# Value projections of the mixers and the retention, computed token by token with the activations stationary

## The reference, cut to what matters

```python
# first block, layer 1: retention, 4 heads, dv = 512, latent and context tokens (512 in all)
p = h @ w_in
q, k, v, g = split(p)                     # v: (heads, tokens, 512)
scores = einsum('bhid,bhjd->bhij', q, k) * intra
y = einsum('bhij,bhje->bhie', scores, v) + ...
# second block, both layers: mixer
hq, hf, hi, hg, aq, ak, av, ga, gb = split(h @ w_in[l])
v_a = hi.reshape(b, t, 8, 128)            # values of the gated scan (hgrn2)
v_b = heads(av)                           # values of 3 x 4 attention heads of width 128
o_a = hgrn2_chunk_scan(q_a, k_a, v_a, log_f)
o_b = sum over groups of alpha * (softmax(q_b k_b^T) v_b)
```

## Time and profile before

| | |
|---|---|
| runs | 3542.81, 3546.66, 3550.40 us; median 3546.66 |
| profiled execution | 3541.26 us, of which the span in the profile is 3539.5 |
| busy | PE 3431.8 us, DVE 2032.4, ACT 1268.4, POOL 640.2 |
| DMA | 507.9 MB, queue share 48.7% |
| mean granted TensorE clock | 0.99 |

### The profile page before, as it was taken

One profiled execution on the slowest core, in us unless ns is written; L12 is line 12 of the kernel. 1 busy time (PEld: TensorE's weight loads), 2 busy tenths in 40 slices (PEclk: granted clock), 3 DMA queues, 4 the chain that ended last, 5 costly groups with the idle time before them and its releaser, 6 DMA issues.

```text
span 3539.5 us, 55525 instructions
## 1 busy us (share of the span) xinstructions
PE 3431.8 (97%) x22315; PEld 3109.0 (88%) x22315; DVE 2032.4 (57%) x2374; ACT 1268.4 (36%) x1678; POOL 640.2 (18%) x535
## 2 busy tenths in 40 slices
PE   7999999999999999999999999999999999998999
PEld 4888878888888888888999999989999999998999
DVE  3766836657766535545555456855545455864644
ACT  2222223212232124333434344355444444355443
POOL 2212303202221130002222220000323230000222
PEclk9999999999999999999999999999999999999999
DMA  5645504545355433334654654334565655343664
GB/s 195 189 149 155 161 22 123 173 140 175 107 172 167 130 97 89 90 95 140 184 173 140 182 166 138 108 114 131 158 183 165 184 167 155 108 120 93 177 184 143
DMA packets 862994, 507.89 MB, mean 143 GB/s; under 512 B 15060, under 2 KB 843024, under 8 KB 862800
## 3 DMA queue, kind: packets, MB, share of 16 engines
q1 hardware_dynamic: 862432, 503.74, 48.7%
q0 software_dynamic: 368, 1.38, 0.1%
HBM read 504.01 MB, written 1.05 MB: 143 GB/s over the span
## 4 chain that ended last, share of the span: by engine, by line
PE 87%; DVE 5%; ACT 4%; issue 2%; DMA 1%; POOL 0%; SPq 0%; DVEq 0%; POOLq 0%; ACTq 0%
PE bank L578 26%; PE bank L580 25%; PE bank L579 25%; ACT whi_all L1023 2%; PE bank L946 2%; PE bank L589 1%; DVE wlo_all L1271 1%; DVE t_full L1406 1%; PE bank L661 1%; PE bank L800 1%; PE bank L761 1%; PE bank L748 1%; PE bank L850 1%; PE bank L845 1%; DMA raw<-in_w_branch_a 1%
## 5 line engine op out<-in xcount | busy, mean ns | idle before, releaser
L1271 DVE TENSOR_TENSOR wlo_all<-raw,whi_all 128x1024 fp32r<-128x1024 f32 (+3 forms) x768 | 1015.1, 1323 | 972.1 <-ACT whi_all L1023 970.8
L578 PE MATMUL bank<-xn_hi,whi_all 128*128 128x256 f32 (+1 forms) x4608 | 1481.2, 321 | 18.6 <-DVE xn_lo L1395 11.4
L579 PE MATMUL bank<-xn_lo,whi_all 128*128 128x256 f32 (+1 forms) x4608 | 1447.4, 314 | 0.0
L580 PE MATMUL bank<-xn_hi,wlo_all 128*128 128x256 f32 (+1 forms) x4608 | 1447.2, 314 | 0.0
L1023 ACT CAST whi_all<-raw 128x1024 fp32r<-128x1024 f32 (+3 forms) x768 | 836.5, 1090 | 1032.6 <-PE bank L580 988.4
L578 PEld LDWEIGHTS bank<-xn_hi,whi_all 128*128 128x128 f32 x4608 | 882.6, 192 | 83.6 <-DVE xn_lo L1395 13.5
L580 PEld LDWEIGHTS bank<-xn_hi,wlo_all 128*128 128x128 f32 x4608 | 881.8, 191 | 52.3
L579 PEld LDWEIGHTS bank<-xn_lo,whi_all 128*128 128x128 f32 x4608 | 883.0, 192 | 49.5
L578 PE MATMUL bank<-h_hi,whi_all 128*128 128x256 f32 (+1 forms) x1408 | 459.0, 326 | 1.2 <-POOL h_lo L1767 1.2
L580 PE MATMUL bank<-h_hi,wlo_all 128*128 128x256 f32 (+1 forms) x1408 | 454.7, 323 | 0.0
L579 PE MATMUL bank<-h_lo,whi_all 128*128 128x256 f32 (+1 forms) x1408 | 454.4, 323 | 0.0
(11 more groups left out here) (247 smaller groups left out, 2802.2 us busy)
## 6 DMA issues: line engine op xcount, KB each, us to landing
raw<-in_ffn_w_in SPq DMA_DIRECT2D x176, 512.0 KB, 3.9
raw<-in_w_in SPq DMA_DIRECT2D x168, 512.0 KB, 3.8
ada_w<-in_ada_w SPq DMA_DIRECT2D x128, 512.0 KB, 4.0
raw<-in_ffn_w_gate SPq DMA_DIRECT2D x88, 512.0 KB, 3.8
raw<-in_ffn_w_up SPq DMA_DIRECT2D x88, 512.0 KB, 3.9
raw<-in_ffn_w_down SPq DMA_DIRECT2D x32, 768.0 KB, 5.2
raw<-in_ret_w_in SPq DMA_DIRECT2D x48, 512.0 KB, 3.8
raw<-in_ffn_w_out SPq DMA_DIRECT2D x32, 768.0 KB, 5.4
```

Source lines behind the costliest of these rows:

```text
L578: pe.matmul(o, whi[s][:, k, :], hi, start=(k == 0), stop=False)
L579: pe.matmul(o, whi[s][:, k, :], lo, start=False, stop=False)
L580: return pe.matmul(o, wlo[s][:, k, :], hi, start=False, stop=(k == ks - 1))
L1271: tt(wlo[s][:, 0:ks, :], raw[s][:, 0:ks, :], whi[s][:, 0:ks, :].bitcast(F32), ALU.subtract).then_inc(lo_done[s], 1)
```

## The change

- In `ret_v`, `hi` and `att_v` the 128x128 activation blocks are stationary and the weights of two neighbouring slots move together (2 x 128 columns). A pair of slots gives, per token tile, 256 output columns with the tokens on the partitions.
- A pair starts when both slots are ready, and its 48 products (96 in the retention) run before `mm_done` of either slot is signalled. The last product is cut into two of 128 columns, each of which signals one slot.
- In the mixer the first half of a pair's products (k = 0 to 3) is issued in the even unit and the second half in the odd one.
- ACT copies each bank straight to the values' final place. `r_vf`, `vfm`, all transposes of values, their copies and their semaphores are gone. Waits that they carried are put elsewhere. The order of all other side steps is as it was.

```diff
-        for n in range(5):
-            put(HI + 4 * n + 4, "turn", n)
...
+            def pair_ready(s, r):
+                slot_ready(s - 1, r)
+                slot_ready(s, r)
+
+            def values_mm(s, blocks, hi, lo, tiles):
...
+                two = slice(s - 1, s + 1)
+                for t, k in blocks:
+                    b, c0 = s - 1 + 2 * t // tiles, t % (tiles // 2) * 2 * P
+                    o = bank[b][:, c0:c0 + 2 * P]
+                    tok = slice(t * P, (t + 1) * P)
+                    pe.matmul(o, hi[:, k, tok], whi_all[:, two, k, :], start=(k == 0), stop=False)
+                    pe.matmul(o, lo[:, k, tok], whi_all[:, two, k, :], start=False, stop=False)
+                    if (t, k) != (tiles - 1, DC - 1):
+                        pe.matmul(o, hi[:, k, tok], wlo_all[:, two, k, :], start=False, stop=(k == DC - 1))
+                        continue
+                    for i in range(2):
+                        pe.matmul(o[:, i * P:(i + 1) * P], hi[:, k, tok], wlo_all[:, s - 1 + i, k, :], start=False,
+                                  stop=(i == 1)).then_inc(mm_done[s - 1 + i], 1)
...
-                    linear(f"ret_v{h}", pair(xn_hi, xn_lo, 512), 512)
-
-                    pe.wait_ge(rt["vf"], 4 * (h + 1))
-                    for t in range(4):
...
-                        for e in range(4):
-                            mm = pe.transpose(bank[4 + t][:, e * P:(e + 1) * P], r_vf[:, e, t * P:(t + 1) * P], ident[:])
-                        mm.then_inc(rt["vt"], 1)
+                    for s in (1, 3):
+                        pair_ready(s, phases[f"ret_v{h}"]["first"])
+                        values_mm(s, [(t, k) for t in range(4) for k in range(DC)], xn_hi, xn_lo, 4)
...
+                    if ph in ("hi", "att_v"):
+                        blocks = [(t, k) for k in range(DC) for t in range(2)]
+                        if s % 2:
+                            values_mm(s, blocks[DC:], xn2_hi, xn2_lo, 2)
+                        else:
+                            pair_ready(s + 1, p["first"] + it)
+                            values_mm(s + 1, blocks[:DC], xn2_hi, xn2_lo, 2)
+                        return
...
-                def turn(i):
...
-                        for s in range(SLOTS):
-                            mm = pe.transpose(bank[6 + t][:, s * P:(s + 1) * P], vfm[:, s, t * P:(t + 1) * P], ident[:])
...
-                        act.copy(r_vf[:, s, :], bank[s][:]).then_inc(rt["vf"], 1)
-                        act.wait_ge(rt["vf"], 4 * h + s + 1)
-                        act.nop().then_inc(bank_free[s], 1)
+                        i = s % 2
+                        act.copy(r_v[:, 2 * i:2 * i + 2, (s - i) * P:(s - i + 2) * P],
+                                 bank[s][:].rearrange("p (t e) -> p t e", t=2)).then_inc(bank_free[s], 1)
...
-                        act.copy(vfm[:, s, :], bank[s][:, 0:SEQ]).then_inc(att["vf"], 1)
...
+                        n, t = n0 + c // SLOTS, s % 2
+                        dst = g_v(t, n) if n < 2 else a_v[t][:, n - 2, :, :]
+                        act.copy(dst[:, s - t:s - t + 2, :], bank[s][:, 0:SEQ].rearrange("p (c e) -> p c e", c=2))\
+                            .then_inc(bank_free[s], 1)
...
-                    for t in range(4):
-                        dve.wait_ge(rt["vt"], 4 * h + t + 1)
-                        dve.tensor_copy(r_v[:, t, :], bank[4 + t][:]).then_inc(rt["v"], 1)
```

More of the change, by code:

```diff
@@ L188, in mixer_order @@
         side = [[] for _ in units]
-        QK, HI, HG = 16, 40, 60
+        QK, HG = 16, 60
         def put(u, *item):
@@ L330, in build @@
         r_k = at("r_k", [P, 2, 512], 82)
-        r_vf = at("r_vf", [P, 4, 512], 86)
         r_yn = at("r_yn", [P, 2, 512], 86)
@@ L356, in build @@
         a_qk = at("a_qk", [P, 24, SEQ], 76)
-        vfm = at("vfm", [P, 4, SEQ], 100)
         a_s = at("a_s", [P, 1152], 104)
@@ L428, in build @@
         f_a, f_ae, f_aed, f_b, f_hi, f_lo = [sem(f"four_{n}") for n in ("a", "a_sb", "a_sb_dve", "b", "hi", "lo")]
-        rt = {k: sem(f"ret_{k}") for k in ("qk", "kctx", "vf", "vt", "v", "dm", "expo", "s", "p", "y", "var", "root",
+        rt = {k: sem(f"ret_{k}") for k in ("qk", "kctx", "dm", "expo", "s", "p", "y", "var", "root",
                                            "yn", "yt", "z", "zlo")}
-        att = {k: sem(f"att_{k}") for k in ("vf", "vt", "v", "sq", "ss", "rt", "rr", "sp", "tk", "rope", "s", "mx",
+        att = {k: sem(f"att_{k}") for k in ("sq", "ss", "rt", "rr", "sp", "tk", "rope", "s", "mx",
                                             "ex", "rs", "p", "pt", "pte", "o", "ohi", "olo")}
@@ L790, in do_retention @@
                     pe.wait_ge(rt["kctx"], 2 * (h + 1))
-                    pe.wait_ge(rt["v"], 4 * (h + 1))
                     for j in range(4):
+                        if h:
+                            pe.wait_ge(rt["yn" if j < 2 else "z"], 2 * h)
                         for c in range(2):
@@ L796, in do_retention @@
                         mm.then_inc(rt["s"], 1)
+                    for s in range(SLOTS):
+                        pe.wait_ge(bank_free[s], phases[f"ret_v{h}"]["first"] + 2)
                     pe.wait_ge(rt["p"], 4 * (h + 1))
@@ L859, in sum_, with values_taken @@
                     row_sum(c % 12, 11, 7, a_sq[c % SLOTS], att["ss"])
[L861 to L867, removed]
+                def values_taken(ph):
+                    p = phases[f"{ph}{l}"]
+                    for s in range(SLOTS):
+                        pe.wait_ge(bank_free[s], p["first"] + p["rounds"] + 1)
                 def spread(i):
                     pe.wait_ge(att["rr"], 2 * l + i // 6 + 1)
-                    bank6_free()
+                    if 12 * l + i:
+                        pe.wait_ge(att["tk"], 12 * l + i)
                     row_spread(2 * i % 12, 6, 0, a_rr[i // 6])
                     row_spread(2 * i % 12 + 1, 6, 1, a_rr[i // 6]).then_inc(att["sp"], 1)
-                    spreads[0] += 1
-                def turn(i):
[L878 to L883, removed]
-                        for s in range(SLOTS):
-                            mm = pe.transpose(bank[6 + t][:, s * P:(s + 1) * P], vfm[:, s, t * P:(t + 1) * P], ident[:])
-                        mm.then_inc(att["vt"], 1)
-                    turns[0] += 2
                 def scores(hh):
@@ L892, in scores @@
                         pe.wait_ge(att["rope"], 12 * (l + 1))
-                        pe.wait_ge(att["v"], 10 * (l + 1))
                         pe.wait_ge(hg["oe"], 4 * (l + 1))
@@ L925, in attend @@
                         pe.wait_ge(hg["hm"], 4 * (l + 1))
+                        values_taken("att_v")
                     if n:
@@ L962, in values @@
                         pe.wait_ge(hg["xe"], 4 * (l + 1))
-                        pe.wait_ge(att["v"], 10 * l + 4)
+                        values_taken("hi")
                     for h in range(4 * half, 4 * half + 4):
@@ L976, in hsum @@
                     pe.wait_ge(hg["oe"], 4 * l + 4)
-                    pe.wait_ge(att["v"], turns[0])
+                    pe.wait_ge(att["rt"], 2 * (l + 1))
                     for h in range(HH):
@@ L987, in hspread @@
                     row_spread(2 * j + 1, 7, 1, g_rr[:]).then_inc(hg["sp"], 1)
-                steps_ = dict(unit=unit, sum=sum_, spread=spread, turn=turn, scores=scores, turn_probs=turn_probs,
+                steps_ = dict(unit=unit, sum=sum_, spread=spread, scores=scores, turn_probs=turn_probs,
                               attend=attend, pairs=pairs, cross=cross, values=values, hsum=hsum, hspread=hspread)
@@ L1128, in values @@
                         if h and s == 0:
-                            act.wait_ge(rt["yt"], 2 * h)
-                            act.wait_ge(rt["zlo"], h)
-                        act.copy(r_vf[:, s, :], bank[s][:]).then_inc(rt["vf"], 1)
-                        act.wait_ge(rt["vf"], 4 * h + s + 1)
-                        act.nop().then_inc(bank_free[s], 1)
+                            act.wait_ge(rt["y"], 2 * h)
+                        i = s % 2
+                        act.copy(r_v[:, 2 * i:2 * i + 2, (s - i) * P:(s - i + 2) * P],
+                                 bank[s][:].rearrange("p (t e) -> p t e", t=2)).then_inc(bank_free[s], 1)
                     stream(f"ret_v{h}", values)
@@ L1160, in evacuate @@
                     def evacuate(s, c, r):
-                        n = 5 * l + n0 + c // SLOTS
-                        if s == 0 and n:
-                            act.wait_ge(att["vt"], 2 * n)
-                        act.copy(vfm[:, s, :], bank[s][:, 0:SEQ]).then_inc(att["vf"], 1)
-                        act.wait_ge(att["vf"], 4 * n + s + 1)
-                        act.nop().then_inc(bank_free[s], 1)
+                        n, t = n0 + c // SLOTS, s % 2
+                        dst = g_v(t, n) if n < 2 else a_v[t][:, n - 2, :, :]
```

(6 more changed lines are left out.)

## The result

| | before | after |
|---|---|---|
| median of the runs | 3545.19 us (4 runs) | 3569.28 us (4 runs, 3567.89 to 3574.10) |
| ratio to before | | 1.0068, 95% interval 1.0051 to 1.0086 |
| span of the profiled execution | 3539.5 | 3566.9 (+27.4) |
| u40 to u61, layer 0 / layer 1 | 102.1 / 100.3 | 113.7 / 114.1 |
| retention, heads 1 to 3, each | 68.0 | 66.9 |

The account below looks back on a forecast made before the run. TensorE was taken as the bound, busy 97%, with DVE and ACT close behind in the mixer. Retention -4.1 and mixers +32.6 gave +28.5 us, so 3575 us on the median, range 3548 to 3598.

Parts of the forecast that it names:

- The central claim: Mixer: DVE and ACT run close behind TensorE, so when they may start can matter more than TensorE's work.
- Rivals 1 and 3: Whole kernel: not slower because side steps have slack, 3515 us, chance 0.11; new matmul form dear, 3598 or above, chance 0.09.
- Retention, -4.1: Four retention heads: removed stretch -2.55, narrower matmuls +1.28, cut halves +0.24, so -1.03 us a head.
- Here the pairs should wait for nothing: Retention: pairs of slots find their splits done in time, so no waiting time was added.
- Turns and their waits, 7.7 a layer: Mixer, removed per layer: five turns of 8 transposes, 4.3 us, and two waits for ACT's copies, 1.8 and 1.6.
- gaps 22.9: Mixer, per layer: eight new TensorE waits for late ACT and DVE side steps, 22.9 us together.
- E+1.84: Mixer: DVE's lo of the even slot starts 1.84 us after the pair's end on TensorE.
- u54: Mixer: spread 9 waits for bank 6 from rope 8, behind squares(1) on ACT, a gap of 3.7 us.
- The halves: Last product of a pair cut into two of 128 columns, 0.12 us each, adding 0.12 a pair.
- four falls added and two taken off: Mixer, per layer: clock falls of 1.8 us each, four new ones 7.2 us, two removed ones 3.6.
- Mixers forecast +32.6: Both mixer layers: gaps 22.9, clock 7.2 and halves 1.2, less 15.0 removed, +16.3 us a layer.
- Rival 2: Mixers: gaps come but half as large, 15 instead of 30 us a layer, 3545 us; chance 0.10.

Follow-up runs that it names:

- mix_only: The changed kernel with the retention's part of the diff taken back, so only the mixers have the new form; 3570.27 us, 1.0071 of the kernel before.
- late_signal: The kernel before, with mm_done of even slots in hi and att_v signalled only near the end of the odd unit; 3601.06 us, ratio 1.0153.
- defer: The changed kernel with ACT's and DVE's even units in hi and att_v done at the odd units; 3531.68 us, 0.9965 of the kernel before.
- defer_h0: defer, with DVE splitting slot 1 before the rope at ret_qk of head 0; 3528.26 us, 0.9955 of the kernel before.
- defer_dve: The changed kernel with even units in hi and att_v put off to the odd ones on DVE alone; 3542.49 us, 0.9993 of the kernel before.

## Why the prediction was right, and where it was off

**What bounds.** The central claim held: a change of when ACT and DVE may start matters more than a change of TensorE's work. mix_only puts the loss in the mixers; late_signal makes it from the old matmuls by the signal alone; defer undoes it with the new matmuls and the signal left as it is. Rivals 1 and 3 are out: the gaps came, and the pace is 0.119.

**Retention, -4.1: measured -1.1.** Heads 1 to 3 are each 1.11 us shorter (68.03 to 66.92 from scores to scores), where I had 1.03. The failed step is "Here the pairs should wait for nothing", for head 0. There ret_qk runs across its four slots, so all four mm_done come within a few microseconds of the end, and the pair needs slot 1, whose split stands behind the rope. From the end of the crossed part to the scores, head 0 takes 38.9 us instead of 36.7, +2.2 instead of -1.0. defer_h0 shows the cause by shortening it.

**Turns and their waits, 7.7 a layer.** They are gone, L885 and its waits alike.

**What comes, gaps 22.9: measured 20.0.** The mis-sized term is E+1.84: ACT's copy no longer waits for its own end, and every meeting that hangs on the first lo came 0.3 us sooner. u54 was off by more, 0.8: two such copies lie on its path (0.4), and the four operations of squares start 0.48 apart and not 0.55 (2322.12 to 2324.03 on ACT, 0.3 in all). The halves make a pair 0.05 longer (0.17 against 0.12) instead of 0.12.

**Clock.** I had four falls added and two taken off in each layer. Windows of PE behind the gaps at u43, u47, u51 and u54 of layer 0:

```profile
2261.81:2266.81 5.00, 5.00 (x21) 0.50 0.71 210
2287.04:2291.04 4.00, 4.00 (x21) 0.57 0.45 131
2309.68:2313.68 4.00, 4.00 (x27) 1.00 0.44 131
2327.53:2331.53 4.00, 4.00 (x18) 0.60 0.45 131
```

Three falls came and not four, in layer 1 behind the same three gaps; the first was longer than I counted, and behind the gap of 2.6 at u51 there was none. My two taken off hold for layer 0 alone. In layer 1 of the kernel before, the clock did not fall behind the second of the waits that I used, 1.82 us ahead of L850:

```profile
3136.61:3140.61 4.00, 4.00 (x29) 1.00 0.41 120
```

So my choice of "3 us or more" as the border had no support in the rows. PEclk over the stretch fell from 0.97 and 0.98 to 0.94. By a ledger of layer 0, 102.1 less 3.7, 3.4 and 4.0 (five turns at 0.80) for what went, plus 20.0 and 0.5, is 111.5; it took 113.7, so about 2.2 is left for the clock, where I had 3.6. The windows agree with this estimate: length times what PEclk lacks of 1 is 2.5 + 1.7 + 1.6 now and 1.7 + 1.7 before, 2.4 more.

**Sum.** Mixers forecast +32.6, measured +11.6 and +13.8, together +25.4. Layer 1 lost more because it had one fall of the clock less before, and as many after. With the retention that is +24.3, near the +24.1 of the medians; the other 3 us between the two profiled executions lie outside these stages. The forecast was 4 us high: the mixers were 7 too dear, the retention 3 too cheap.

Rival 2, half of what I counted, didn't come: 20.0 of the 22.9 us of gaps did. That the total is within 4.4 us of the forecast is in part luck, since the errors of the mixers and of the retention have opposite signs.

## What to carry to other kernels

When two units are merged so that their end is signalled once, list all that other engines run behind the first unit's signal, not only what takes its result. Moving the wait behind the side steps (a few lines an engine here) can be worth more than the change that called for it. Work out each meeting from the signal: sum on the late engine against sum on the waiting one; here that gave eight gaps to within 0.8 us each. And look at the first round apart from the others: where it is ordered in another way, a cover that holds everywhere else may not hold there.

## What the runs showed of the hardware that was not expected

- The two halves of a cut product, 128 columns each and each with its own weight load, start 0.06 us apart, half of the 0.120 of a 256-column product and less than the 0.11 of a transpose of the same width. What follows starts 0.11 after the second. Windows of L656 alone, the first ending just before the start of the second half and the other just behind it:

```profile
2246.06:2246.13 0.07, 0.06 (x1) 1.00 0.00 0
2246.06:2246.14 0.08, 0.07 (x2) 1.00 0.00 0
```

  A long stream of such halves is not shown to keep that pace. The weight loads around them, the last with the sum that follows, are 0.11 to 0.12 apart (two in the 0.23 us from 2245.95 to 2246.18), and the sum starts 0.06 after its load does:

```profile
2245.95 0.31 PEld L656 LDWEIGHTS bank<-wlo_all,xn_hi 128*128 128x128 f32 x2
2246.18 0.30 PEld L864 LDWEIGHTS bank<-silu_g,mod 128*128 128x128 f32 x2
```

- The same gap does not always cost the same. In defer_dve, values(0) waits 2.39 us in both layers. Windows of PE behind it, layer 1 and layer 0:

```profile
3117.54:3121.84 4.30, 4.30 (x16) 0.60 0.52 149
2296.30:2298.94 2.64, 2.64 (x17) 1.00 0.34 99
```

In layer 1 the clock fell to 1.2 GHz for a part and the same step took 4.30 us; in layer 0 it did not, 2.64. The next large wait, 2.75 us at u54 in both layers, repeats this: over the 4 us behind it PEclk is 0.68 in layer 1 and 1.00 in layer 0. And behind the wait at u43, 3.15 us in both, it is 0.50 and 0.63. Together the layers' stretches differ by 4.4 us. Which gap is followed by a fall, and for how long, can't be told from its length alone.
